# A two-layer transformer block on one core: other orders of loads, modulation steps and variance in the mix stage, and a third expert piece split early

## The reference

```
mod = silu(c) @ w_ada[l] + b_ada[l]
shift1, scale1, gate1, shift2, scale2, gate2 = split(mod, 6)
h = rms_norm(x, norm1_g[l]) * (1 + scale1) + shift1
proj = h @ w_in[l]
attn_out = mla_group(...)                        # 4 heads of 128 values
conv_out = silu(layer_norm(conv(gated) + conv_b) * g + b)   # 512 channels
x = x + gate1 * (concat(attn_out, conv_out) @ w_out[l])
h2 = rms_norm(x, norm2_g[l]) * (1 + scale2) + shift2
aff = softmax(h2 @ w_router[l])                  # 16 experts
gate, idx = top_k(aff.T, 128)                    # each expert takes 128 tokens
ye = (silu(xe @ w_gate[e]) * (xe @ w_up[e])) @ w_down[e] * gate, xe = h2[idx]
x = x + gate2 * scatter_add(ye, idx)
```

## Time and profile before

| | |
|---|---|
| median of three runs | 3834.46 us (3832.05 to 3835.71) |
| profiled execution, own time | 3834.46 us |
| its span, first to last instruction | 3832.6 us |
| mean granted TensorE clock | 0.952 of 2.4 GHz |
| TensorE, VectorE, ScalarE, GpSimd busy | 92%, 64%, 42%, 25% |
| mix stages, second half from | 528.95 and 1778.08 us |
| routing stages, norm from | 613.38 and 1862.52 us |

### The profile page before, as it was taken

The page is one execution under the profiler, slowest core; times in us unless marked ns, Lnnn a source line. Parts: engine busy times, 40 slices in busy tenths (PEclk is TensorE's granted clock), DMA queues, the critical chain, the costliest instruction groups (busy, mean ns, idle before and its releaser), DMA issues. The chain is left out here.

```text
span 3832.6 us, 46620 instructions
## 1 busy us (share of the span) xinstructions
PE 3516.2 (92%) x16424; PEld 2821.5 (74%) x16424; DVE 2433.8 (64%) x2269; ACT 1610.0 (42%) x1642; POOL 974.7 (25%) x609
## 2 busy tenths in 40 slices
PE   7997989899999599799989999969987989999998
PEld 6746975788888474697568888858865778888886
DVE  6977776788898497777678898854047232222224
ACT  5124442688888411444268888823134110000001
POOL 1203200111111121330011111025433445453632
PEclk9998999899999799899989999979997989999999
DMA  4100047799999210004779999931100211111111
GB/s 174 35 14 13 12 151 285 292 395 392 403 395 354 77 40 14 13 12 139 283 297 393 397 400 395 363 121 50 49 9 9 79 61 60 38 60 39 46 47 55
DMA packets 134192, 619.15 MB, mean 162 GB/s; under 512 B 17761, under 2 KB 35553, under 8 KB 84961
## 3 DMA queue, kind: packets, MB, share of 16 engines
q1 hardware_dynamic: 124896, 584.61, 39.7%
q0 software_dynamic: 9216, 33.56, 3.4%
HBM read 571.45 MB, written 41.94 MB: 160 GB/s over the span
## 5 line engine op out<-in xcount | busy, mean ns | idle before, releaser
L1813 DVE TENSOR_TENSOR ex_lo<-ex_raw,ex_hi 128x2048 fp32r<-128x2048 f32 x380 | 863.2, 2291 | 125.0 <-ACT ex_hi L1763 124.9
L1763 ACT CAST ex_hi<-ex_raw 128x2048 fp32r<-128x2048 f32 x380 | 724.2, 1914 | 164.5 <-PE psum L1725 143.0
L1723 PE MATMUL psum<-ex_hi,xe_hi 128*128 128x512 f32 x1024 | 404.1, 395 | 1.3 <-DVE xe_lo L1818 1.3
L1724 PE MATMUL psum<-ex_lo,xe_hi 128*128 128x512 f32 x1024 | 400.8, 391 | 0.0
L1725 PE MATMUL psum<-ex_hi,xe_lo 128*128 128x512 f32 x1024 | 400.7, 391 | 0.0
L2582 DVE TENSOR_TENSOR ff_full<-psum,ff_full 128x1024 f32<-128x1024 f32 x22 | 26.9, 1225 | 408.5 <-PE psum L431 408.5
L516 DVE SCALAR_TENSOR_TENSOR mix<-y,lcols,mix 128x1024 f32<-128x1024 f32 x176 | 268.2, 1525 | 5.7
L1723 PEld LDWEIGHTS psum<-ex_hi,xe_hi 128*128 128x128 f32 x1024 | 193.5, 189 | 41.3 <-issue 2.0
L1725 PEld LDWEIGHTS psum<-ex_hi,xe_lo 128*128 128x128 f32 x1024 | 193.4, 189 | 40.5
L431 PE MATMUL psum<-hn_hi,up_hi 128*128 128x512 f32 x704 | 218.3, 392 | 5.0 <-DVE hn_lo L1936 4.8
L1724 PEld LDWEIGHTS psum<-ex_lo,xe_hi 128*128 128x128 f32 x1024 | 193.6, 189 | 38.9
(11 more groups left out here) (421 smaller groups left out, 7451.7 us busy)
## 6 DMA issues: line engine op xcount, KB each, us to landing
ex_raw<-w_experts_dram SPq DMA_DIRECT2D x384, 1024.0 KB, 7.2
mix<-w_ada_dram SPq DMA_DIRECT2D x64, 512.0 KB, 4.2
up_raw<-w_gate_up_dram SPq DMA_DIRECT2D x44, 512.0 KB, 3.3
rt_ada<-w_ada_dram SPq DMA_DIRECT2D x32, 512.0 KB, 5.7
in_raw<-w_in_dram SPq DMA_DIRECT2D x24, 512.0 KB, 3.4
p_raw<-w_in_dram SPq DMA_DIRECT2D x24, 512.0 KB, 3.3
wd_raw<-w_down_dram SPq DMA_DIRECT2D x11, 1024.0 KB, 6.9
ada_w<-w_ada_dram SPq DMA_DIRECT2D x8, 1024.0 KB, 13.5
```

The lines of the kernel that those rows point to most:

```text
L1723: pe.matmul(bank(out), x_hi, h[:, k, :], start=first, stop=False)
L1724: pe.matmul(bank(out), x_hi, r[:, k, :], start=False, stop=False)
L1763: act.copy(hi[j % PARTS][:], raw[j % RAW][:]).then_inc(w_hi, 1)
L1813: dve.tensor_tensor(lo[j % PARTS][:], raw[j % RAW][:], hi[j % PARTS][:].bitcast(F32), ALU.subtract).then_inc(w_lo, 1)
```

## The change

In the mix stage the low part of tile 2 goes ahead of an addition. The variance sums and `spread` both go behind tile 2's first half. `tile_steps` and with it the place of reduction 2 change, the steps go behind low part and square sum, and SyncE's order of loads is another. In the routing stage three pieces are split early instead of two, and their refills go ahead of the modulation loads 4 and on and of the row writes. In the experts' stage the gathered rows are split ahead of the remaining pieces.

```diff
@@ -53,7 +53,7 @@
 PIECES = 12
 RAW = 6
 PARTS = 4
-SPLIT_EARLY = 2
+SPLIT_EARLY = 3
 N_MOD = 6
 ADA_RING = 8
 LATE_RING = 4
@@ -1088,7 +1088,7 @@
                 ada_used, reduced, mods_done = sem("lo_ada_used"), sem("lo_reduced"), sem("lo_mods_done")
                 n_steps = LATE_CHUNKS * DT
                 before_add = DT
-                tile_steps = [1, 1, 1, 5, 5, 5, 6]
+                tile_steps = [0, 3, 3, 5, 5, 5, 3]
                 assert before_add + sum(tile_steps) == n_steps
                 ends = [before_add + sum(tile_steps[:n + 1]) for n in range(DT - 1)]
 
@@ -1114,16 +1114,24 @@
                         for n in range(LO_BUFS):
                             load_tile(n)
                         load_ada(0, LATE_RING)
-                        for n in range(LO_BUFS, 2 * LO_BUFS):
+                        load_tile(LO_BUFS)
+                        load_tile(LO_BUFS + 1)
+                        load_ada(LATE_RING, LATE_RING + 4)
+                        load_tile(LO_BUFS + 2)
+                        load_ada(LATE_RING + 4, LATE_RING + ends[2])
+                        for n in range(LO_BUFS + 3, DT):
                             load_tile(n)
-                        load_ada(LATE_RING, LATE_RING + before_add)
-                        load_tile(2 * LO_BUFS)
-                        load_ada(LATE_RING + before_add, LATE_RING + ends[1])
-                        load_tile(2 * LO_BUFS + 1)
-                        load_ada(LATE_RING + ends[1], n_steps)
+                            load_ada(LATE_RING + ends[n - 4], min(LATE_RING + ends[n - 3], n_steps))
+                        load_ada(LATE_RING + ends[DT - 4], n_steps)
 
                     @block.tensor
                     def _(pe):
+                        def variance():
+
+                            pe.wait_ge(added, CT - 1)
+                            token_sums(pe, var_cols, acc).then_inc(var_sum, 1)
+                            spread(pe, spread_banks, diag, diag_done).then_inc(spread_done, 1)
+
                         def reduce_mod(c):
                             pe.wait_ge(ada_used, (c + 1) * DT)
                             mod_columns(pe, mod_psum[:, c * DT:(c + 1) * DT], mod_acc[c % 2]).then_inc(reduced, 1)
@@ -1143,12 +1151,10 @@
                             pe.wait_ge(lo_split, n + 1)
                             if n == LO_BUFS - 1:
                                 pe.wait_ge(centred, CT)
-                                pe.wait_ge(added, CT - 1)
-                                token_sums(pe, var_cols, acc).then_inc(var_sum, 1)
                             for k in range(HEADS):
                                 pe.wait_ge(lo_done, k + 1)
                                 take(n, k)
-                        spread(pe, spread_banks, diag, diag_done).then_inc(spread_done, 1)
+                        variance()
                         for n in range(LO_BUFS):
                             if n == LO_BUFS - 1:
                                 pe.wait_ge(scaled, CT)
@@ -1213,8 +1219,8 @@
                                                      op0=ALU.mult, op1=ALU.add).then_inc(centred, 1)
                             if j >= 2:
                                 add(j - 1)
+                        split_low(2)
                         add(CT - 1)
-                        split_low(2)
                         mod_steps(0, 2)
                         dve.wait_ge(root, 1)
                         dve.reciprocal(stat[:, 1, :], stat[:, 0, :]).then_inc(rstd, 1)
@@ -1240,15 +1246,12 @@
                             dve.wait_ge(w_used, n + 1)
                             dve.scalar_tensor_tensor(out=x[:, n, :], in0=banks(tile_banks[n % LO_BUFS]), scalar=gate[:, n:n + 1],
                                                      in1=x[:, n, :], op0=ALU.mult, op1=ALU.add).then_inc(x_added, 1)
-                            first = ends[n - 1] if n else before_add
-                            if n < DT - 1:
-                                mod_steps(first, first + 1)
                             if n and n + LO_BUFS < DT:
                                 split_low(n + LO_BUFS)
                             if n >= 2:
                                 add_square(n - 1)
                             if n < DT - 1:
-                                mod_steps(first + 1, ends[n])
+                                mod_steps(ends[n - 1] if n else before_add, ends[n])
                         add_square(DT - 1)
                         dve.wait_ge(reduced, LATE_CHUNKS)
                         dve.tensor_tensor(modl[:, 3:N_MOD, :], mod_psum[:, DT:4 * DT].rearrange("p (n j) -> p n j", j=DT),
@@ -1462,13 +1465,13 @@
                             load_piece(sp, raw[j], 0, j).then_inc(loaded[j], 16)
                         with sp.Fori(0, TB) as i:
                             sp.dma_start(moe_rows[bass.ds(i * P, P), :], zero_row[:]).then_inc(zeroed, 16)
+                        for j in range(SPLIT_EARLY):
+                            load_ahead(sp, 0, j, pieces)
                         load_ada(NEXT_RING, NEXT_RING + 3)
                         for t in range(TB):
                             sp.wait_ge(row_copied[t % 2], t // 2 + 1)
                             sp.dma_start(h2_rows[t * P:(t + 1) * P, :], rows[:, t % 2, :]).then_inc(rows_out[t % 2], 16)
                             load_ada(NEXT_RING + 3 + 2 * t, min(NEXT_RING + 5 + 2 * t, 2 * DT))
-                        for j in range(SPLIT_EARLY):
-                            load_ahead(sp, 0, j, pieces)
                         sp.wait_ge(zeroed, 16 * TB)
                         for b in range(2):
                             sp.wait_ge(rows_out[b], 16 * TB // 2)
@@ -1799,9 +1802,9 @@
                             output(e)
 
                         act.sem_inc(ye_done, 2)
+                        rows_hi(0)
                         for j in range(SPLIT_EARLY, PARTS):
                             split_hi(0, j)
-                        rows_hi(0)
                         with act.Fori(0, last) as e:
                             expert(e, True)
                         expert(last, False)
@@ -1843,9 +1846,9 @@
                                     if more:
                                         rows_lo(e + 1)
 
+                        rows_lo(0)
                         for j in range(SPLIT_EARLY, PARTS):
                             split_lo(0, j)
-                        rows_lo(0)
                         with dve.Fori(0, last) as e:
                             expert(e, True)
                         expert(last, False)
```

## The result

| | before | after |
|---|---|---|
| median of four runs | 3834.07 us (3832.05 to 3835.71) | 3874.18 us (3870.51 to 3877.77) |
| ratio | | 1.0105, 95% interval 1.0088 to 1.0122 |
| profiled execution, own time and span | 3834.46, 3832.6 | 3873.78, 3872.0 |
| mean granted TensorE clock | 0.952 | 0.946 |

The change makes the kernel 40 us slower. The prediction said 29 us slower, 3863.5, with a range that ended at 3874.0: the direction held, the size did not, and the median lies just above the range. The page of the kernel after begins like this; TensorE is busy for 18 us more than in the earlier trace rows with the same number of instructions, which is time at the lower clock, and the rest of the 39.4 us of span is idle time.

The account below looks back on a forecast made before the run. TensorE, busy 92% of the span, was taken as the bound, losing time where it stands still or runs slower. Mix 6.5 plus routing 8.0 is 14.5 us per layer, twice 29: 3834.5 + 29 = 3863.5 us, range 3845 to 3874.

Parts of the forecast that it names:

- Part 1: Mix stage, variance sums behind tile 2's first half: two idle stretches change places, -0.1 us per layer.
- Part 2: Mix stage, modulation steps and loads: TensorE waits 5.1 us before reduction 2, then loses 1.5 us at lower clock, per layer.
- Part 4: Start of the experts, gathered rows split before remaining pieces: the order was hidden, so nothing changes.
- step 24: Mix stage, VectorE's modulation step needed by reduction 2: done at 589.7 us, while tile 5 ends at 584.6.
- Part 3: Routing stage, third piece split early and refills loaded first: 8.0 us slower per layer.
- row 4: Routing stage, modulation row whose load queues behind 3.15 MB of refills: 7.6 us later, landing at 658.3 us.
- A: Whole kernel, all waits as summed: 3863.5 us, own range 3852 to 3875, chance 0.60.
- D: Mix and routing stages, no wait grows past its cover: change does nothing, 3834 us, chance 0.07.
- E: Experts start sooner and the other waits stay covered: 3825.5 us, chance 0.05.
- I take 1.5, bounds 0 and 3.0: Mix stage, lower clock behind the wait before reduction 2: costs 1.5 us per layer, bounds 0 and 3.0.
- 7.6 + 2.0 - 1.6: Routing stage per layer: row 4 later by 7.6 us, half-clock restart 2.0, slack before the search's end takes 1.6 back.
- the sum of the bounds: Whole kernel, all terms at their bounds, 5.35 to 22.2 us per layer: 3845 to 3879 us.

Follow-up runs that it names:

- 3: Kernel before with only the variance order changed: low part of tile 2 ahead of one addition, sums and spread behind tile 2's first half; 3834.89 us, ratio 1.0000.
- 4: Kernel before with the changed mix stage, but SyncE's tile and modulation loads in the old order; 3834.78 us, ratio 0.9995.
- 5: Kernel before with the changed mix stage's loads and steps, but reduction 2 behind tile 6 as before; 3841.97 us, ratio 1.0019.
- 11: Kernel before with the changed mix stage, tile 7's load moved directly behind tile 6's, ahead of modulation loads; 3845.51 us, ratio 1.0027.
- 8: Kernel before with only the experts' order changed: gathered rows split ahead of pieces 2 and 3; 3835.99 us, ratio 0.9998.
- 7: Kernel before with two pieces split early, their refills ahead of modulation loads 4 and on, gathered rows first; 3846.50 us, ratio 1.0028.
- 12: Kernel before with the changed mix stage, plus 32 unused matmuls of 128x512 ahead of TensorE's wait before reduction 2; 3856.5 us, ratio 1.0061.
- 6: Kernel before with three pieces split early, refills behind the row writes as before, gathered rows first; 3840.47 us, ratio 1.0011.
- 2: Kernel before with the whole changed mix stage, routing and experts' stages as before; 3859.44 us, ratio 1.0065.

## Why the direction was right and the size wrong

**Mechanisms.** The waits of Parts 1, 2 and 4 came as told: the idle stretches changed places (3), step 24 came late through tiles 6 and 7 in SyncE's queue (4, 5, 11), and the order of the gathered rows gave nothing (8). In Part 3 row 4 was 7.83 us later against 7.6, and 7 shows that the price, bytes ahead over 412 GB/s, was about right (4.8 for 5.1). Of the cases, A happened, whose own range of 3852 to 3875 holds the median; D and E needed waits that stayed within their cover.

**The step that failed** is Part 2, in the sizes of two of its terms, and through them the top of the range.

*"Behind such a stall the clock is down ... I take 1.5, bounds 0 and 3.0."* From reduction 2 to the end of the stage it is 32.35 and 32.83 us in the kernel after, 28.8 with a warm start (12): 3.6 and 4.0 us, above the upper bound. The forecast wait of 5.1 us was close to the 4.92 us of the row that gave the price, so the price was not read off too short a wait. And the kernel after shows that a longer wait alone doesn't make it dearer. These are its windows behind 6.64 us idle, where plain matmuls of 128x512 follow, and behind the 6.01 us of layer 1, where reduction 2 with its 16 matmuls of 128x1 comes first; the window behind 7.82 us, again with the reduction, stands above (7.70 us at 0.52):

```profile
528.00:531.70 3.70, 3.69 (x9) 2.93 (x10) 3.70 (x4) 3.67 (x4) 0.00 (x0) 0.51 0.08 32
1861.20:1869.90 8.70, 8.64 (x29) 7.53 (x30) 7.91 (x8) 1.06 (x1) 0.00 (x0) 0.52 0.85 298
```

The slow stretch is 3.7 us behind 6.64, 8.7 us behind 6.01 and 7.7 us behind 7.82. In 11 it is 7.0 us behind a wait of only 2.15 us, again with a reduction first. The price was read at a place with other work behind the wait, and carried over. That the reduction in front makes the difference is not shown: no run changed only that. The upper bound was read too small as well. It took the 6 us from 700 to 706 in the earlier trace rows, but the slow stretch behind those 6.57 us idle runs from 697.8 to 706.2, in the kernel before:

```profile
697.80:706.20 8.40, 7.73 (x22) 6.08 (x23) 2.04 (x3) 2.90 (x5) 1.15 (x2) 0.50 0.79 305
```

Half of 8.4 is 4.2 us, and a bound of that size would have held the 3.6 and 4.0. (At the same place in layer 1 the stretch is 5.4 us, at 0.50.) In two layers the term is 7.6 - 3.0 = 4.6 us short.

*"issue 0.3, landing 4.5 ... bring step 24 to 589.7. TensorE waits 5.1 us for it."* Measured 7.82 and 6.01 us. Tile 7 landed after 6.5 us in layer 0: the landing of 4.5 was read off a load with two others issued in the 3.5 us ahead of it, and here five were issued in 5.2 us. That these five made it longer is a reading of the queue; no run tested it by itself. 2.0 us of longer landing and 0.7 us of later issue (575.81 for 575.1) are the 2.7 us of layer 0, which is above the upper bound of 6.5 too. In layer 1 step 24 is as late, but TensorE itself comes 1.6 us later, for the reason below, and waits 0.9 us more than forecast. Over both layers the term is 2.7 + 0.9 = 3.6 us short.

*Not seen at all:* waits of 0.61 and 0.85 us before reduction 1, and in layer 1 a start of tile 5 at half clock behind it, pairs of matmuls of 1.05 us from 1842.67 to about 1846, half of 3.2 us. Together 3.1 us. With 4.6 and 3.6 this makes 11.3 of the 11.8 us by which the mix stages missed.

**Routing, 8.0 against 6.67 and 6.33.** Forecast were 7.6 + 2.0 - 1.6. Measured in layer 0: row 4 is 7.83 us later and the restart costs 2.4 (1.7 on row 4, 0.7 on the transposes), so ScalarE's last copies end 10.2 us later; the slack to the search takes 1.6 back, as forecast; and 1.9 us come back that nobody forecast, 1.4 of them from the short matmuls. 10.2 - 1.6 - 1.9 = 6.7. In layer 1 row 4 is 7.2 us later, the restart costs 1.3, the slack takes 1.7 back and the end of the stage 0.5: 6.3. TensorE stood for 5.68 us before row 4 and not for the forecast's 8.2, since its own rows ahead of the wait came 2.7 us later; that was covered, and cost nothing. So the total of this part is near for a sound main term, and by luck for two that nobody saw: one was hidden and the other, in layer 0, gave time back. GpSimd's hold on VectorE costs 2.4 us per layer when it stands alone (6). Here it is hidden: row 4 starts when its load lands, and TensorE's wait for the product, 1.69 us, lies ahead of that. The Trainium skill, TensorE: Matmul & The Clock Gate, HAM oscillation, says that the burst behind a long DMA wait starts cold; the trace agrees, with 3.57 us for row 4 in place of 1.88. (The 4.92 us that the prediction sets beside the same page were a wait for VectorE, not for a DMA.)

**The range.** Its top, 3874, lay below the sum of the bounds, 3879, and the median fell between them. The prediction left that out as a tail. But the restart came out above its upper bound in both layers, and the wait above its own in layer 0. The two belong together in one way: where there is no wait there is no restart. They don't grow together, as those windows show.

**Open.** The 1.6 us outside the four stages, the 4 us between trace and timing in 5, and what sets the length of a slow stretch.

## What to carry to other kernels

A load's place in a queue is set by what the entries ahead of it wait for: tile 7 stood behind a modulation load that needed 19 steps, which needed tile 6, and a chain like this turns a few microseconds of lateness into a stall as soon as another edit asks for the result one tile sooner; each edit alone cost nothing or little. Price a stall on TensorE as the wait plus the slow stretch behind it. Take the price from rows where the same kind of work follows, measure the slow stretch from its first slow matmul to its last, and keep the range wide: here it cost 1.7 to 4.1 us behind waits of 2.1 to 7.8 us with a reduction in front, and the longer wait was not the dearer. And if an order gains nothing, look for the work that now stands in front of what it freed: two modulation steps moved into the idle stretch turned the variance order from no gain into 1.8 us of each mix stage.

## What the runs showed of the hardware

**A VectorE product of two SBUF tiles waits for GpSimd's instruction.** Two products of 128x64 took 0.36 us with GpSimd idle, 4.36 us beside one subtraction of 128x2048 (4.5 us), and 1.84 us beside subtractions of 128x512 (1.26 us each), the last two ending within about 0.2 us of a GpSimd instruction's end. The Trainium skill, SBUF — State Buffer, SBUF: two separate sides, tells of a port pair that VectorE and GpSimd share under a lock held for the whole instruction; the trace agrees, with 4.36 against 0.36 us, and cutting GpSimd's instruction in four gave 2.5 us per layer back. Other VectorE instructions in that time, a reduction out of PSUM of 0.29 us and a reciprocal of 0.20 us, were not held.

**How long the lower clock lasts behind a wait did not follow the length of the wait.** Right behind each stretch the granted clock was 0.96 or more.

| run, layer | idle before, us | first behind it | slow stretch, us, at granted clock |
|---|---|---|---|
| before, 0 | 4.92 | matmuls of 128x512 | 3.5 at 0.51 |
| before, 0 | 6.57 | 8 transposes, then 0.63 us idle | 8.4 at 0.50 |
| before, 1 | 6.18 | the same | 5.4 at 0.50 |
| after, 0 | 6.64 | matmuls of 128x512 | 3.7 at 0.51 |
| after, 0 | 7.82 | reduction, 16 of 128x1 | 7.7 at 0.52 |
| after, 1 | 6.01 | reduction | 8.7 at 0.52 |
| 2, layer 0 | 5.94 | reduction | 8.7 at 0.51 |
| 2, layer 1 | 7.36 | reduction | 7.7 at 0.51 |
| 11, layer 0 | 2.15 | reduction | 7.0 at 0.51 |
| 11, layer 1 | 2.13 | reduction, at full clock | then 3.8 at 0.55 |

Short waits before reduction 1 don't order themselves by length either. Behind 0.61 us (after, layer 0) and 0.98 us (5, layer 1) the clock stayed at 1.00. Behind 0.85 us (after, layer 1) and 0.42 us (2, layer 0) the reduction still ran at or near full clock, and then the clock fell for about 3.5 us. These are single places, not a law.
